# Mamba heads of a hybrid decoder layer: the table of cumulated decays on 128 rows in place of 48

## The reference, cut to what matters

```python
dt = softplus(dt_raw + dt_bias)
a = dt * A                                # one number for each token and head
a_cs = cumsum(a, axis=-1)                 # over the tokens
decay_in = exp(segsum(a))                 # exp(a_cs[l] - a_cs[s]) for s <= l, otherwise 0
y_diag = einsum('bclgn,bcsgrp->bclgrp', CB[:, :, None] * decay_in, Xdt)
...
```

## Time and profile before

| | us |
|---|---|
| median of 3 runs | 581.5 |
| lowest and highest run | 580.88, 581.5 |
| span of the profiled execution | 579.7 |
| PE busy | 562.8 (97%) |
| PEld busy | 512.7 (88%) |
| DVE busy | 323.1 (56%) |
| ACT busy | 288.8 (50%) |
| POOL busy | 50.3 (9%) |

### The profile page before, as it was taken

One profiled execution on the slowest core, in us unless ns is written; L12 is line 12 of the kernel. 1 busy time (PEld: TensorE's weight loads), 2 busy tenths in 40 slices (PEclk: granted clock), 3 DMA queues, 4 the chain that ended last, 5 costly groups with the idle time before them and its releaser, 6 DMA issues.

```text
span 579.7 us, 9569 instructions
## 1 busy us (share of the span) xinstructions
PE 562.8 (97%) x3744; PEld 512.7 (88%) x3744; DVE 323.1 (56%) x434; ACT 288.8 (50%) x463; POOL 50.3 (9%) x86
## 2 busy tenths in 40 slices
PE   5999999999999999999999999989999999999995
PEld 5999999999999879997888788879999999999993
DVE  3654554555455584877565546674545455554544
ACT  4544444344444375767465755364534443453433
POOL 1000040000000020603242002010000000000001
PEclk9999999999999999999999999999999999999999
DMA  8945596655555837546323224433666554566601
GB/s 252 310 128 198 157 301 223 217 183 179 165 154 189 275 118 211 160 145 218 97 86 110 72 74 147 144 128 100 211 217 217 159 188 158 154 210 217 216 2 73
DMA packets 69448, 98.01 MB, mean 169 GB/s; under 512 B 1828, under 2 KB 55392, under 8 KB 69424
## 3 DMA queue, kind: packets, MB, share of 16 engines
q1 hardware_dynamic: 68576, 95.21, 50.7%
q0 software_dynamic: 848, 2.47, 1.4%
HBM read 96.62 MB, written 1.05 MB: 168 GB/s over the span
## 4 chain that ended last, share of the span: by engine, by line
PE 93%; DVE 2%; ACT 1%; DMA 1%; POOL 1%; issue 0%; SPq 0%; POOLq 0%; DVEq 0%; ACTq 0%
PE bank L1101 28%; PE bank L1102 28%; PE bank L1103 28%; DMA raw<-in_ffn_w 1%; PE bank L1230 1%; PE bank L1362 1%; PE bank L1364 1%; ACT z_silu L476 1%; PE bank L1375 1%; PE bank L1376 1%; PE bank L1404 1%; POOL mean_sq L363 1%; DVE x L782 1%; PE bank L1403 1%; PE bank L1374 0%
## 5 line engine op out<-in xcount | busy, mean ns | idle before, releaser
L770 DVE TENSOR_TENSOR w_lo<-raw,w_hi 128x1024 fp32r<-128x1024 f32 x176 | 210.7, 1225 | 149.2 <-ACT w_hi L452 148.6
L452 ACT ACTIVATE w_hi<-raw 128x1024 fp32r<-128x1024 f32 x176 | 179.7, 1054 | 112.2 <-PE bank L1103 71.2
L1101 PE MATMUL bank<-hT_hi,w_hi 128*128 128x256 f32 x736 | 208.6, 283 | 0.0
L1103 PE MATMUL bank<-hT_hi,w_lo 128*128 128x256 f32 x736 | 208.3, 283 | 0.0
L1102 PE MATMUL bank<-hT_lo,w_hi 128*128 128x256 f32 x736 | 208.2, 283 | 0.0
L1101 PEld LDWEIGHTS bank<-hT_hi,w_hi 128*128 128x128 f32 x736 | 141.1, 192 | 1.6
L1102 PEld LDWEIGHTS bank<-hT_lo,w_hi 128*128 128x128 f32 x736 | 141.1, 192 | 1.4
L1103 PEld LDWEIGHTS bank<-hT_hi,w_lo 128*128 128x128 f32 x736 | 141.1, 192 | 0.0
L1101 PE MATMUL bank<-w_hi,hT_hi 128*128 128x512 f32 (+1 forms) x192 | 69.6, 362 | 0.4 <-DVE w_lo L770 0.3
L1101 PE MATMUL bank<-w_hi,gu_hi 128*128 128x512 f32 x176 | 69.2, 393 | 0.3
L1102 PE MATMUL bank<-w_lo,gu_hi 128*128 128x512 f32 x176 | 69.0, 392 | 0.0
(11 more groups left out here) (164 smaller groups left out, 425.0 us busy)
## 6 DMA issues: line engine op xcount, KB each, us to landing
raw<-in_ffn_w SPq DMA_DIRECT2D x63, 1024.0 KB, 5.5
raw<-in_w_in SPq DMA_DIRECT2D x16, 1024.0 KB, 5.6
raw<-in_w_out SPq DMA_DIRECT2D x6, 1024.0 KB, 5.0
raw<-in_ffn_w SPq DMA_DIRECT2D x6, 512.0 KB, 7.5
x<-in_x SPq DMA_DIRECT2D x4, 256.0 KB, 3.9
out_x<-normed SPq DMA_DIRECT2D x4, 256.0 KB, 2.1
norm_w<-in_ffn_norm SPq DMA_DIRECT2D x1, 512.0 KB, 6.1
norm_w<-in_mix_norm POOLq DMA_DIRECT2D x1, 512.0 KB, 5.5
```

What stands on the lines that cost most here:

```text
L452: act.activation(by_tile(dst) if columns else dst, src, ACT.Copy).then_inc(hi_ready, 1)
L770: dve.tensor_tensor(lo, src, hi, ALU.subtract).then_inc(half_ready, 1)
L1101: pe.matmul(dst, lhs[0], rhs[0], start=start, stop=False, skip_group_check=True)
L1103: return pe.matmul(dst, lhs[1], rhs[0], start=False, stop=stop, skip_group_check=True)
```

## The change

The table, the selecting column and the cleared tile get 128 rows (for `cs_rows`, which holds the table before its transpose, 128 columns). Rows 48 to 127 hold zeros on both sides of the product. The dt product and its transposes keep their 48 rows; only the constant's name changes there. The working tile of the rotation is laid over `gu`, a tile of the feed-forward parts of the same size.

```diff
-CS_ROWS = 3 * SH
+DT_ROWS = 3 * SH
...
-        select_r = sb("select_r", [CS_ROWS, SH], f32r)
+        select_r = sb("select_r", [P, SH], f32r)
...
-        cs_rows = sb("cs_rows", [P, TT, CS_ROWS])
-        csT = sb("csT", [CS_ROWS, 384], f32r)
+        cs_rows = sb("cs_rows", [P, TT, P])
+        csT = sb("csT", [P, 384], f32r)
...
-        rot_t = sb("rot_t", [P, TT, HEADS, ROT])
+        rot_t = gu[:, :].rearrange("p (t h r) -> p t h r", t=TT, h=HEADS)
...
-            act.activation(select_r[:, :], cst[0:CS_ROWS, C_SEL:C_SEL + SH], ACT.Copy).then_inc(consts_r, 1)
+            act.activation(select_r[:, :], cst[:, C_SEL:C_SEL + SH], ACT.Copy).then_inc(consts_r, 1)
...
-                dve.tensor_copy(cs_rows[:, :, 2 * SH:], cs).then_inc(cs_tok_ready, 1)
+                dve.tensor_copy(cs_rows[:, :, 2 * SH:3 * SH], cs).then_inc(cs_tok_ready, 1)
...
-                step(dve.tensor_copy(csT[:, :], bank[0:CS_ROWS, 7, 0:384]))
-                lo = slice(2 * SH, CS_ROWS)
+                step(dve.tensor_copy(csT[:, :], bank[:, 7, 0:384]))
+                lo = slice(2 * SH, 3 * SH)
...
-                    last = pe.transpose(bank[0:CS_ROWS, 7, j * P:(j + 1) * P], cs_rows[:, t, :], ident)
+                    last = pe.transpose(bank[:, 7, j * P:(j + 1) * P], cs_rows[:, t, :], ident)
...
-                pe.matmul(b[:, 0:384], select_r[:, h:h + 1].to_broadcast([CS_ROWS, P]), csT[:, :],
+                pe.matmul(b[:, 0:384], select_r[:, h:h + 1].to_broadcast([P, P]), csT[:, :],
                           start=True, stop=False, skip_group_check=True)
```

More of the change, by code:

```diff
@@ L111, in build @@
         wdt = sb("wdt", [P, KD, SH])
-        wdt_parts = sb("wdt_parts", [P, KD, CS_ROWS], f32r)
+        wdt_parts = sb("wdt_parts", [P, KD, DT_ROWS], f32r)
         sumsq = sb("sumsq", [P, 2, 10])
@@ L120, in build @@
         gu_lo = sb("gu_lo", [P, 2, SEQ], f32r)
-        bias_col = sb("bias_col", [CS_ROWS, 1])
-        dtT = sb("dtT", [CS_ROWS, SEQ])
+        bias_col = sb("bias_col", [DT_ROWS, 1])
+        dtT = sb("dtT", [DT_ROWS, SEQ])
         conv_acc = sb("conv_acc", [P, 4, SEQ])
@@ L661, in _ @@
             act.wait_ge(dtT_done, 1)
-            act.activation(dtT[:, :], bank[0:CS_ROWS, 7, 0:SEQ], ACT.Identity, bias=bias_col[:, :]).then_inc(dtT_ready, 1)
+            act.activation(dtT[:, :], bank[0:DT_ROWS, 7, 0:SEQ], ACT.Identity, bias=bias_col[:, :]).then_inc(dtT_ready, 1)
             for m in range(5, MIX_HALVES):
@@ L1250, in dt_product @@
                     h_hi, h_lo = hT(k, slice(0, SEQ))
-                    pe.matmul(bank[0:CS_ROWS, 7, 0:SEQ], wdt_parts[:, k, :], h_hi, start=k == 0, stop=False,
+                    pe.matmul(bank[0:DT_ROWS, 7, 0:SEQ], wdt_parts[:, k, :], h_hi, start=k == 0, stop=False,
                               skip_group_check=True)
@@ L1261, in dt_transposes @@
                 for t in range(TT):
-                    last = pe.matmul(bank[:, 6, t * SH:(t + 1) * SH], dtT[:, tok(t)], cst[0:CS_ROWS, C_SEL:C_SEL + SH],
+                    last = pe.matmul(bank[:, 6, t * SH:(t + 1) * SH], dtT[:, tok(t)], cst[0:DT_ROWS, C_SEL:C_SEL + SH],
                                      start=True, stop=True)
```

## The result

The changed kernel takes 576.53 us (median of 4 runs, 575.76 to 577.03) against 581.5: a ratio of 0.9913 with a 95% interval from 0.9899 to 0.9927. It is faster by 5.0 us. The forecast was 575.3 with a range of 574.5 to 577.3.

A forecast was written before the change was run, and what follows sets the result against it. TensorE's own matmul sequence was taken as the bound, stopping at both edges of each 48-row matmul. Gains 0.77 + 5.4 make 6.2 us: span 579.7 - 6.2 = 573.5, plus 1.8 for launch and end, 575.3; range 574.5 to 577.3.

The forecast's parts named there:

- Fewer than 128 rows: At TensorE's seams: what they share is a contraction over fewer than 128 rows; both seams of L1362 would go.
- The pair behind m = 19: From L1103 to the next L1101, two decay matmuls with their masks: 1.59 us becomes 0.82, gain 0.77.
- The 14 other heads: Decay matmuls between heads: a head goes from 1.29 us to 0.905, gain 0.385 each, 5.4 in all.
- already has the next matmul's load in it: Reason for taking 6.2 us: the 0.61 of an ssd_out with nothing behind it includes the next load.
- The prediction's lower bound: Each of a head's eight loads takes its own 0.11: head 0.945, gain 0.345, with the pair 5.6 us.
- PE still doesn't wait: At ssd_out(10), PE needs DVE's weigh(10): 1.6 us of slack less three gains of 0.385 leaves 0.4.
- the prediction's own signs of being wrong: L1362's starts staying 0.32 and 0.37 apart, new DVE or POOL waits between 285 and 306, later parts not moving together.
- The third rival: Heads 8 to 11: PE waits for DVE at ssd_out(10) and ssd_out(11), losing at worst 1.2 us; 576.5, chance 0.08.
- What was costed at nothing: Transposes L1285, ACT's and DVE's copies, POOL's clearing, the rotation's tile: each taken as 0, some up to 0.3 us uncovered.
- the seams stay: Around L1362: row count doesn't matter, the stop belongs to broadcast weight or the pair L1362/L1364; 581.5 or 581.8, chance 0.05.
- only one edge closes: Only the edge behind L1362 goes, the broadcast load still starting late: 3.1 us gained, 578.4, chance 0.04.
- The late rotation of k: POOL's rotation, held up further, makes PE wait at L1390 after 3.7 us of slack: slower, 584.8, chance 0.02.

The follow-up runs named there:

- e1: Changed kernel, but the decay matmul L1362 contracts over 48 rows again, all else kept: 581.45 us, ratio 0.9997 against the kernel before.
- e5: Changed kernel with L1362 on 48 rows, both decay_args of a step directly behind chunk_half, each L1362 followed by its mask matmul: 582.17 us.
- e6: Changed kernel with L1362 on 48 rows, both decay_args behind chunk_half, the two L1362 adjacent, then both mask matmuls: 579.03 us.
- e3: Changed kernel, but L1362 contracts over 96 rows: 576.7 us, ratio 0.9916 against the kernel before.

## Why the prediction was right, and where it was off

**The bound.** Right: PE lost time at both edges of the 48-row matmul, and but for one wait nobody else had to be asked. Every part of the reading from the rows held: the open loads, the same seam at L1262, none at L1285's 48 columns. e1 shows that the cause is the contraction's rows, and e5 against e6 that it is the change between row counts. "Fewer than 128 rows" was one step too general (e3).

**The pair behind m = 19.** Forecast 0.77, measured 0.77 (0.78 from the unrounded starts).

**The 14 other heads.** This is the first term that was mis-sized: 0.385 forecast, 0.33 measured, 14 x 0.055 = 0.8 us. The step that failed is the sentence that the 0.61 of `ssd_out(14)` "already has the next matmul's load in it". That 0.61 began behind a matmul of 512 columns, under which the first loads were done, so it holds fewer than six whole load steps. The prediction's lower bound had the mechanism, a load of 0.11 for each of eight matmuls, which gives 0.945 and is close to the 0.97 of the trace; it was worked out and then set aside. The row to look at was `ssd_out(15)`, which has narrow matmuls on both sides and so holds six whole load steps: it takes 0.68, from 316.01 to the next record at 316.69, and 0.68 + 0.175 + 0.12 = 0.975.

**The wait at ssd_out(10).** This is the second: 0.4 us, forecast at nothing. "PE still doesn't wait" was wrong, and a new wait for DVE between 285 and 306 was one of the prediction's own signs of being wrong; it shows in the row of the loads. The third rival, DVE at the bound, came true at one of its two places and with a third of its 1.2 us. The prediction named the place and left 0.4 of slack. Two things used it up. DVE's stretch was no fixed block: from `ssd_add(0)` to the end of `weigh(10)` it took 7.0 us before, and 7.8 now (291.57 to half of the 1.95 behind 298.43). And what needs the result is the load, which elsewhere starts 0.23 ahead of the matmul from whose start the slack was counted (274.58 and 274.81). With the two terms, 6.2 - 0.8 - 0.4 = 5.0, against 4.97 in the stretch and 5.0 between the medians.

**The range.** Both misses go the same way, and the measured 576.53 would have lain just outside the forecast's own 574.5 to 576.5. It is inside the stated range because the DVE rival had been taken in. That end was added up as 576.5 + 0.6, which is 577.1 and not 577.3; the result lies below either.

**What was costed at nothing.** The transposes L1285 start 0.12 behind their neighbour as before, and 0.45 from there the second matmul behind starts, as before (255.56 and 256.01). DVE's copy into `csT` takes 551 ns (549 before), POOL's clearing 0.31 us in place of 0.18, under the wait for constants. e1 bounds all of it together: -0.1 us, within an interval of about 0.6 either way.

**The rivals.** That the seams stay and that only one edge closes are out: both loads are under cover. The late rotation of k went the other way, as below.

## What to carry to other kernels

When TensorE is the bound, look for matmuls that contract over 48 or 64 rows among full ones (fewer rows were not tried): each way in and out costs some 0.39 us here, which a weight load that starts together with its own matmul, after idle time put down to "issue", gives away. Padding both operands with zeros to 96 or 128 rows cost nothing that shows in the matmul itself (0.18 us for 384 columns, between the 0.12 for 256 and the 0.23 for 512). Putting the narrow ones next to each other in pairs gave half of the gain. When a load comes under cover, price what remains by the loads if the neighbours have few columns, and take the distances from a place with the same neighbours.

## What the runs showed of the hardware that was not expected

- 96 rows run like 128, and 64 like 48 (576.7, 576.53, 581.44 and 581.45 us).
- A record of 256 columns in float32 lies 0.22 us from the next, one of float32r 0.12.
- POOL and DVE seem to stretch each other, and which of them pays seems to depend on how they meet. This is read from which instructions overlap; no run takes either engine's work away. The rotation of k took 8.05 us before, with its first instruction held for 3.79 while DVE's `ssd_gate(0)` (L987) took 1.28:

```profile
298.87 1.28 DVE L987 TENSOR_TENSOR normed<-normed,z_silu 128x512 f32<-128x512 f32 x2
```

In the changed kernel the stretch begins with another offset, POOL's eight instructions take 6.11 (293.71 to 299.82) and DVE's gate 1.81:

```profile
293.71 0.38 POOL L375 TENSOR_TENSOR gu<-k_tok,cst 128x64 f32<-128x64 f32 x1 [14.78 <-ACT k_tok L597]
...
299.37 0.45 POOL L378 TENSOR_TENSOR k_tok<-k_tok,gu 128x128 f32<-128x128 f32 x1
...
295.43 1.81 DVE L987 TENSOR_TENSOR normed<-normed,z_silu 128x512 f32<-128x512 f32 x2
```

It is not the tile over `gu`: in e1, with the same tile and the old pace, the first instruction is held again, for 3.78 us.
